# Products and their parts for two v tiles at a time, one-hots in two instructions, gate factors on ScalarE

## The reference

```
s_top, i_top = top_k(keys . (x @ w_q), 16)          # per head, two halves
best, pos = top_k(s_top[0] + s_top[1], 16)          # 16 of 16384 experts per head, 8 heads
g = softmax(best)
h = gelu(x . u[expert])
out = sum over the chosen experts of (g * h) * v[expert]
```

## Time and profile before

| what | us |
|---|---|
| median of 3 timed runs | 1654.39 |
| lowest and highest of them | 1652.92, 1654.40 |
| the profiled execution, span from its first to its last instruction | 1652.1 |
| PE busy | 1634.0 |
| DVE busy | 1246.6 |
| ACT busy | 646.1 |

### The profile page before, as it was taken

How to read it: one execution, slowest core, us unless ns; L and a number is a source line. 1 busy time by engine, 2 the same in 40 slices (tenths; PEclk the granted TensorE clock), 3 DMA queues, 4 the chain that set the end, 5 groups by cost and what they waited for, 6 DMA issues and landing times.

```text
span 1652.1 us, 23515 instructions
## 1 busy us (share of the span) xinstructions
PE 1634.0 (99%) x9093; PEld 1456.3 (88%) x9093; DVE 1246.6 (75%) x2357; ACT 646.1 (39%) x1006; POOL 464.2 (28%) x218
## 2 busy tenths in 40 slices
PE   9999999999999999999999999999999999999997
PEld 7898987888888999999999999999998888888886
DVE  3023456444799999998888789998998888888887
ACT  5333345543222343345545333333333433333332
POOL 4432223343224557410000223333333122222100
PEclk9999999999999999999999999999999999999999
DMA  5431112126112558588787999999999999999961
GB/s 204 157 140 52 52 54 77 45 83 230 52 52 82 182 176 295 190 330 279 242 281 237 350 390 394 380 388 370 358 375 375 390 384 375 375 363 386 399 242 70
DMA packets 135135, 407.05 MB, mean 246 GB/s; under 512 B 10352, under 2 KB 71024, under 8 KB 113776
## 3 DMA queue, kind: packets, MB, share of 16 engines
q1 hardware_dynamic: 116592, 271.32, 45.1%
q0 software_dynamic: 18432, 134.23, 20.7%
HBM read 360.94 MB, written 44.56 MB: 245 GB/s over the span
## 4 chain that ended last, share of the span: by engine, by line
PE 81%; DVE 17%; DMA 1%; issue 1%; ACT 0%; DVEq 0%; SPq 0%
PE bank L1303 24%; PE bank L1305 24%; PE bank L1304 24%; PE bank L1585 3%; PE bank L1422 2%; DVE idx L1084 1%; DVE idx L1076 1%; DVE val L1075 1%; DVE val L1083 1%; DVE tmp L1077 1%; PE bank L1437 1%; DVE prod L1140 1%; PE bank L1393 1%; PE bank L1385 1%; DVE prod L1149 1%
## 5 line engine op out<-in xcount | busy, mean ns | idle before, releaser
L1303 PE MATMUL bank<-xhi,whi 128*128 128x384 f32 (+1 forms) x1408 | 499.5, 355 | 2.3 <-ACT hout L824 1.8
L1305 PE MATMUL bank<-xhi,wlo 128*128 128x384 f32 (+1 forms) x1408 | 492.7, 350 | 0.0
L1304 PE MATMUL bank<-xlo,whi 128*128 128x384 f32 (+1 forms) x1408 | 492.0, 349 | 0.0
L629 POOL DMA_INDIRECT uvb<-in_uv,eidx x128 | 201.6, 1575 | 697.8 <-DVE acc L1191 667.4
L803 ACT ACTIVATE whi<-raw 128x1024 fp32r<-128x1024 f32 x256 | 270.2, 1057 | 254.4 <-PE bank L1305 228.1
L1169 DVE TENSOR_TENSOR wlo<-raw,whi 128x1024 fp32r<-128x1024 f32 x218 | 265.9, 1221 | 78.9 <-ACT whi L803 78.2
L1305 PE MATMUL bank<-whi,alo 128*128 128x512 f32 x768 | 299.5, 390 | 0.0
L1304 PE MATMUL bank<-wlo,ahi 128*128 128x512 f32 x768 | 299.4, 390 | 0.0
L1303 PE MATMUL bank<-whi,ahi 128*128 128x512 f32 x768 | 298.7, 389 | 0.0
L1303 PEld LDWEIGHTS bank<-xhi,whi 128*128 128x128 f32 x1408 | 264.5, 188 | 18.8 <-issue 3.9
L1305 PEld LDWEIGHTS bank<-xhi,wlo 128*128 128x128 f32 x1408 | 264.3, 188 | 15.6
(11 more groups left out here) (202 smaller groups left out, 1848.2 us busy)
## 6 DMA issues: line engine op xcount, KB each, us to landing
raw<-in_u SPq DMA_DIRECT2D x128, 512.0 KB
raw<-in_uv SPq DMA_DIRECT2D x128, 512.0 KB
g_scratch<-stage SPq DMA_DIRECT2D x48, 512.0 KB, 5.1
gl<-g_scratch SPq DMA_DIRECT2D x32, 768.0 KB
raw<-in_w_in SPq DMA_DIRECT2D x22, 1024.0 KB, 4.8
h_scratch<-hout SPq DMA_DIRECT2D x88, 192.0 KB, 5.3
hl<-h_scratch SPq DMA_DIRECT2D x22, 768.0 KB, 10.1
raw<-in_w_q SPq DMA_DIRECT2D x6, 1024.0 KB, 4.7
```

Source lines behind the costliest of these rows:

```text
L629: nc.gpsimd.indirect_dma_start(out=uvb[:, k % UVB, :], out_offset=None, in_=a["uv"][:, :], in_offset=bass.IndirectOffsetOnAxis(ap=eidx[:, ...
L1303: mm(out, lh, rh, start=first, stop=False)
L1304: mm(out, lh, rl, start=False, stop=False)
L1305: return mm(out, ll, rh, start=False, stop=last)
```

## The change

It makes four edits. (1) `product`, `high_a` and `product_low` treat two v tiles p and p + 1 in one instruction of 768 elements instead of two of 384. The pair's product is put in `PAIR_STEP`: for p below 40 this is two steps after the u tile of p + 1. (2) ACT's `high_a` of a pair is issued in ACT's turn two steps ahead of DVE's, where it was three, and DVE's `product_low` comes two steps after the product, where it was one. (3) `one_hots` compares both index rows in one instruction and multiplies by both weight rows in one. (4) The gate factor of the gathered experts is applied by ACT with two instructions of one element for each partition, where DVE did it with one of two elements; DVE's `sums` waits for both.

```diff
+PAIR_STEP = []
+for p in range(0, NT, 2):
+    at_step = U_POS[v_tile(p + 1)] + 2 if p < FUSED else V_POS[p] - 1
+    PAIR_STEP.append(max(PAIR_STEP[-1:] + [at_step]))
-    at_step = U_POS[v_tile(p)] + 4 if p < FUSED else V_POS[p] - 1
...
                 act.wait_ge(dot_done, 2 * j + 2)
-                nc.scalar.activation(hgel[:, 2 * j:2 * j + 2], hd[:, 2 * j:2 * j + 2], ACT.Gelu).then_inc(dot_gelu, 1)
+                if j == 0:
+                    act.wait_ge(w_done, 1)
+                nc.scalar.activation(hgel[:, 2 * j:2 * j + 2], hd[:, 2 * j:2 * j + 2], ACT.Gelu).then_inc(gel_step, 1)
+                act.wait_ge(gel_step, j + 1)
+                for k in (2 * j, 2 * j + 1):
+                    nc.scalar.activation(hd[:, k:k + 1], hgel[:, k:k + 1], ACT.Copy, scale=wg[:, k:k + 1]).then_inc(dot_gelu, 1)
             def high_a(t):
-                act.wait_ge(a_done, t + 1)
+                act.wait_ge(a_done, t + 2)
                 if t >= 4:
-                    act.wait_ge(v_done, t - 3)
-                nc.scalar.activation(ahi[:, t % 4, :], af[:, t % 4, :], ACT.Copy).then_inc(a_hi, 1)
+                    act.wait_ge(v_done, t - 2)
+                nc.scalar.activation(ahi[:, t % 4:t % 4 + 2, :], af[:, t % 4:t % 4 + 2, :], ACT.Copy).then_inc(a_hi, 2)
...
-                for p in products_in(s + 3):
+                for p in pairs_in(s + 2):
                     high_a(p)
...
             def sums(j):
-                dve.wait_ge(dot_gelu, j + 1)
-                ks = slice(2 * j, 2 * j + 2)
-                step(V.tensor_tensor(hd[:, ks], hgel[:, ks], wg[:, ks], ALU.mult))
+                dve.wait_ge(dot_gelu, 2 * j + 2)
...
-                V.tensor_tensor(e2[:, b % 2, :, :, :], numbers, per_token(1), ALU.is_equal)
-                if b >= 1:
-                    dve.wait_ge(e_done, b)
-                step(V.tensor_tensor(e1q[:, :, :, :], numbers, per_token(0), ALU.is_equal))
-                V.tensor_tensor(e1w[:, b % 2, 0, :, :, :], e1q[:, :, :, :], per_token(2), ALU.mult)
-                V.tensor_tensor(e1w[:, b % 2, 1, :, :, :], e1q[:, :, :, :], per_token(3), ALU.mult).then_inc(e_done, 1)
+                numbers = iota2[:, :, :].unsqueeze(1).to_broadcast([P, 8, P, 2])
+                step(V.tensor_tensor(e12[:, b % 2, :, :, :, :].rearrange("p n g e t -> p (n g) e t"), numbers, per_token(0), ALU.is_equal))
+                ones = e12[:, b % 2, 0, :, :, :].unsqueeze(1).to_broadcast([P, 2, 4, P, 2])
+                V.tensor_tensor(e1w[:, b % 2, :, :, :, :].rearrange("p n g e t -> p (n g) e t"), ones.rearrange("p n g e t -> p n g (e t)"), per_token(2), ALU.mult).then_inc(e_done, 1)
...
             def product(p):
                 if p < FUSED:
-                    dve.wait_ge(h_gelu, n + 1)
-                    h = hout[:, n % 4, :]
+                    dve.wait_ge(h_gelu, n + 2)
+                    h = hout[:, n % 4:n % 4 + 2, :]
...
             def product_low(p):
-                dve.wait_ge(a_hi, p + 1)
+                dve.wait_ge(a_hi, p + 2)
...
-                for p in products_in(s - 1):
+                for p in pairs_in(s - 2):
                     product_low(p)
```

More of the change, by code:

```diff
@@ L115, in v_tile, with pairs_in @@
     return (FIRST_FUSED + p) % NT
-PRODUCT_STEP = []
-for p in range(NT):
-    at_step = U_POS[v_tile(p)] + 4 if p < FUSED else V_POS[p] - 1
-    PRODUCT_STEP.append(max(PRODUCT_STEP[-1:] + [at_step]))
-def products_in(step):
-    return [p for p in range(NT) if PRODUCT_STEP[p] == step]
+PAIR_STEP = []
+for p in range(0, NT, 2):
+    at_step = U_POS[v_tile(p + 1)] + 2 if p < FUSED else V_POS[p] - 1
+    PAIR_STEP.append(max(PAIR_STEP[-1:] + [at_step]))
+def pairs_in(step):
+    return [p for p in range(0, NT, 2) if PAIR_STEP[p // 2] == step]
 BW = S + 3 + 2 * P
@@ L282, in program @@
         arena.phase(at_work)
-        pickT = arena.buf("pickT", [P, 4, DT], F16)
+        pickT = arena.buf("pickT", [P, NB, 4, 8], F16)
         iota2 = arena.buf("iota2", [P, P, 2], F16)
-        e2 = arena.buf("e2", [P, 2, 4, P, 2], F16)
-        e1q = arena.buf("e1q", [P, 4, P, 2], F16)
+        e12 = arena.buf("e12", [P, 2, 2, 4, P, 2], F16)
         e1w = arena.buf("e1w", [P, 2, 2, 4, P, 2], F16)
@@ L562, in _ @@
                     sp.dma_start(ln2b[:, :], a["ln2_b"].partition_broadcast(P)).then_inc(ln2_in, 16)
-                for p in products_in(s):
+                for p in [p + 1 for p in pairs_in(s)]:
                     if p % 4 == 3:
@@ L1220, in product @@
                         dve.wait_ge(h_in[n // 4 % 2], 16 * (n // 8) + 16)
-                    h = hl[:, n // 4 % 2, n % 4, :]
-                V.tensor_tensor(af[:, p % 4, :].rearrange("p (s t) -> p s t", s=SETS), h.rearrange("p (s t) -> p s t", s=SETS),
-                                gl[:, p // 4 % 2, :, p % 4, :], ALU.mult).then_inc(a_done, 1)
+                    h = hl[:, n // 4 % 2, n % 4:n % 4 + 2, :]
+                V.tensor_tensor(af[:, p % 4:p % 4 + 2, :].rearrange("p n (s t) -> p n s t", s=SETS),
+                                h.rearrange("p n (s t) -> p n s t", s=SETS),
+                                gl[:, p // 4 % 2, :, p % 4:p % 4 + 2, :].rearrange("p s n t -> p n s t"),
+                                ALU.mult).then_inc(a_done, 2)
             def product_low(p):
-                dve.wait_ge(a_hi, p + 1)
-                V.tensor_tensor(alo[:, p % 4, :], af[:, p % 4, :], ahi[:, p % 4, :].bitcast(F32), ALU.subtract).then_inc(a_lo, 1)
+                dve.wait_ge(a_hi, p + 2)
+                two = slice(p % 4, p % 4 + 2)
+                V.tensor_tensor(alo[:, two, :], af[:, two, :], ahi[:, two, :].bitcast(F32), ALU.subtract).then_inc(a_lo, 2)
             def norm_last(c, part):
@@ L1272, in _ @@
                     dots(j)
-                for p in products_in(s):
+                for p in pairs_in(s):
                     product(p)
@@ L1279, in _ @@
                     dve.wait_ge(pt_done, 3)
-                    step(V.tensor_copy(pickT[:, 0, :], bank[0][:, 0:DT]))
-                    step(V.tensor_copy(pickT[:, 1, :], bank[1][:, 0:DT]))
-                    step(V.tensor_scalar(pickT[:, 2, :], bank[2][:, 0:DT], W_SCALE, None, ALU.mult))
-                    V.scalar_tensor_tensor(pickT[:, 3, :], bank[2][:, 0:DT], W_SCALE, pickT[:, 2, :], ALU.mult, ALU.subtract).then_inc(pt_out, 1)
+                    by_batch = [bank[n][:, 0:DT].rearrange("p (b t) -> p b t", t=8) for n in range(3)]
+                    step(V.tensor_copy(pickT[:, :, 0, :], by_batch[0]))
+                    step(V.tensor_copy(pickT[:, :, 1, :], by_batch[1]))
+                    step(V.tensor_scalar(pickT[:, :, 2, :], by_batch[2], W_SCALE, None, ALU.mult))
+                    V.scalar_tensor_tensor(pickT[:, :, 3, :], by_batch[2], W_SCALE, pickT[:, :, 2, :], ALU.mult, ALU.subtract).then_inc(pt_out, 1)
                     dve.wait_ge(pt_out, 1)
@@ L1584, in g_quad @@
                     for w in range(2):
-                        last = mm(g_bank(q)[:, i * P:(i + 1) * P], e2[:, b, g, :, t], e1w[:, b, w, g, :, t], start=w == 0, stop=w == 1)
+                        last = mm(g_bank(q)[:, i * P:(i + 1) * P], e12[:, b, 1, g, :, t], e1w[:, b, w, g, :, t], start=w == 0, stop=w == 1)
                 last.then_inc(g_done, 1)
```

8 lines of the change are left out of this document (4 added, 4 removed).

## The result

The changed kernel takes 1664.26 us (median of 4 runs, 1660.07 to 1667.16) against 1654.06 (4 runs, 1652.92 to 1654.4): a ratio of 1.0063, 95% interval 1.0047 to 1.0079. It is slower, and by more than the range of the prediction allowed. The profiled execution is the fastest of the four, 1660.07 us, with a span of 1658.2 against 1652.1.

A forecast was written before the change was run, and what follows sets the result against it. PE was taken as the bound, busy 1634.0 of 1652.1 us. Terms -0.15 + 3.2 + 0.8 gave +3.9, so 1656.0 us for the profiled execution and, 2.3 above, a median of 1658.3 us; range 1653.9 to 1661.5.

The forecast's parts named there:

- The first one-hots: First two one-hot batches and the gathered pairs ahead of them: -0.15 us, between -0.6 and +0.5.
- The start of the products: Steps 91 to 97, first pair product waiting for the gelu of u tile 89: +3.2 us, bounds 0 to some +8.
- PE waits 1.9 us: Before u tile 92, near 970: PE waits for the late gelu of u tile 90, 1.9 us.
- the two signs: Would prove it wrong: gelu of u tile 89 before 963.5, or gate copies costing DVE well over 0.15 us.
- PE waits 1.4 us more: Step 97, near 992: PE waits 1.4 us for `tile_low(97)`, forecast to end at 992.25.
- The end: Last v tiles: `alo` of 126 and 127 comes behind `tile_low(255)`, delaying PE by +0.8 us, bounds +0.4 and +0.95.
- The v-only steps: V-only steps before the end: `product_low` a step later is covered by 5.5 us more room, so nothing was counted.
- The alternating stage: Where u and v tiles alternate: DVE keeps some 3 us of slack at its tightest and catches up slowly.
- From span to median: The runs' median was taken to stand 2.3 us above the profiled span, turning 1656.0 into 1658.3 us.
- the delay that feeds itself: Rival: late `sums` and low parts make loads late, adding one more load wait, 1662 to 1663 us; chance 0.12.
- The wide one-hots: Rival: one-hots run at half rate, each instruction 1.07 us longer, PE waits 64 us, 1718 us; chance 0.04.
- the faster case: Rival: DVE's saving reaches PE's waits at 688 and 723; 1652.7 us, below 1651.1 only without both waits; chance 0.08.

The follow-up runs named there:

- e2: Changed kernel with the one-hot and gate edits undone, so pairs only, against the kernel before: 1658.48 us, ratio 1.0029.
- e3: Kernel before with each `product_low` one step later and nothing paired: 1654.89 us, ratio 1.0012 to the kernel before.
- e9: Changed kernel with its gate edit alone undone (gates multiplied on DVE again): 1657.7 us, ratio 1.0027 to the kernel before.
- e10: e7 with the gate edit undone, leaving pairs and two-instruction one-hots: 1655.14 us, ratio 1.0005 to the kernel before.
- e6: Changed kernel with, in the v-only steps, the high part ahead of `tile_high` and the low part one step earlier: 1657.81 us, ratio 1.0026 to before.
- e4: The changed kernel run again, unaltered: 1660.15 us, ratio 1.0052 to the kernel before.
- e5: Changed kernel with the first pair's product in step 92 instead of 91, its low part in 93: 1659.16 us, ratio 1.0036 to the kernel before.
- e8: Changed kernel without the loads of stored gelu values after the first two (later v tiles use old values): 1660.31 us, ratio 1.0043 to the kernel before.
- e7: Changed kernel with the edits of both e5 and e6: 1654.68 us, ratio 1.0009 to the kernel before.
- e11: e7 with the first four gathered pairs moved to steps 50, 56, 62 and 68: 1650.24 us, ratio 0.9978 to the kernel before.
- e1: Kernel before with only the one-hot and gate edits, no pairs: 1653.87 us, ratio 1.0004 to the kernel before.

## Why the prediction was wrong

**The first one-hots**: -0.15 forecast, -0.28 measured. That is not shown to be right: e2 and e3, in which neither the gates nor the one-hots are changed, have -0.72 and -0.57 at the same step, and e9 and e10, which are the same program up to there, -0.99 and +0.91. A term of 0.15 cannot be read out of single traces that scatter so. What the traces do show are the sizes: two batches take DVE 4.88 us (720.90 to 725.78) where before they took 5.15 and I had 4.9, and a one-hot instruction is 1.22 us (1.23 forecast), an `alo` 0.951 (0.95). PE's later start at step 37 is swallowed by DVE's chain, as I had it. (The change as printed above has `p n g (e t)` in the line of `e1w`; the kernel has `p n (g e t)`. The order of the elements is the same, and the rate was kept.) The Trainium skill, VectorE: DVE Perf Modes, "The TRN2 errata", has many small tiles pay a fixed cost that a large one pays once; the trace agrees, 0.951 us against two of 0.552. Only my total for DVE was too large: 43 us of durations became 25.1 of busy time. Neighbours on the queue overlap by 0.09, and with 224 instructions merged away that much more is lost: some 20 us, by my estimate.

**The start of the products**: +3.2 forecast, 3.42 in the profiled execution, 4.12 to 4.35 in the other three that have this order and the gates' copies. The step "PE waits 1.9 us" was right (1.86, same chain), and so was the end of `tile_low(97)`, 992.25 against 992.16. In part that was luck. The gelu of u tile 89 came at 962.77 and not at 963.49, one of the two signs that I had named as proving me wrong, and the other held too: the copies cost twice what I had. From the gelu's end at 968.01 to `sums` at 968.57 are 0.56 us, where I had 0.38 and before had 0.23: 0.33 a pair instead of 0.15, since a copy takes 0.287 us and not 0.20. The two errors nearly cancel; where the gelu came later, the term is larger by up to 0.9.

"PE waits 1.4 us more" did not happen in this form: the half clock made PE 1.67 later by itself, and it arrived as `tile_low(97)` ended. In this place the clock cost nothing of its own: between 963.40 and 992.16 nothing on DVE's chain waits for PE, and in e2 and e9, where the clock stayed at 1.0, PE stood 0.98 and 0.97 us at step 97 instead.

**The end**: +0.8 forecast, 0.93 measured. Right in kind and nearly in size, and e6 takes it away by the order alone.

**The v-only steps: the first step that failed.** I wrote that there PE has 5.5 us more of cover than at the end, "I count nothing". It cost 2.11 us in the fastest execution, 0.23 to 1.90 in e2, e4, e5 and e9, 0.35 in e8, and 0.00 in all four kernels that put the order back (e6, e7, e10, e11). The cover was computed with tiles that arrive in time. I had two load waits in front of me (4.41 us, and a mean DMA share of 0.95), and used them for the start of the products alone. The order of before let a late load delay only its own tile, which had four steps of room. The new one puts the current product behind that tile, on ACT and on DVE.

**The alternating stage.** I wrote that DVE has "some 3 us of slack at its tightest" there and forecast no wait behind step 97. That held in every trace but e8's, where one load came late and steps 161 and 162 cost 3.90 us.

**From span to median: the second step that failed, and the larger one.** I added 2.3 us, as before. The changed kernel's median lies 6.1 above the profiled span. e4 ran the same kernel again and has its median at 1660.15, 1.9 above its span and inside my range, so this part of the miss is executions that differ. e8's is the only slow one with a trace (1662.81), and its late load explains it. The runs of the changed kernel well above 1660 may be such late loads, but they have no trace, and e2, e6 and e10 do not fit one cause of the scatter: it stays open.

The sum for the profiled execution was 3.9 and is 6.18: -0.13 (first), +0.22 (start), +0.13 (end), +2.11 (v-only) are the 2.3 between them, within rounding. The other 3.8 us of the miss are the median's. Of the rivals, the delay that feeds itself came nearest in size, with another mechanism: load waits passed on by the queue's order, while the delay itself feeds nothing, as e6 shows. The wide one-hots kept their rate, and the faster case failed as reasoned, since DVE's saving mostly fell beside PE's work.

## What to carry to other kernels

Merging two instructions moves the first one's work later and ties it to the second one's input (in e8 the product of one tile waited for the gelu of the next, behind a late load); before counting what the merge saves, list what now stands ahead of it on each queue, above all instructions that wait for a transfer. Cover worked out from a trace where loads land in time is no cover where the DMA share is 0.95: subtract the longest load wait that the trace shows. And where an engine at 74% busy makes the bound engine wait, first see whether its work can stand elsewhere: here four moved pairs gave 4 us, and 288 fewer instructions nothing.

## What the runs showed of the hardware

TensorE's granted clock fell to 0.5 (1.2 GHz) behind some of PE's waits in full-speed stretches, each time for 3.41 us, which made PE 1.5 to 1.7 us later at the next step. It did so behind all five waits of 1.86 to 2.05 us (step 92 in the changed kernel, e4, e6 and e8; step 161 in e8). At step 37 it did not go by length alone: with 2.34 us it fell in the changed kernel, e1, e5 and e7, but not in e4, e6 and e8; with 1.83 or 1.84 it fell in e2 and e3, but not in before, e9 and e10. Behind waits up to 1.66 us it never fell. At step 37 the loss is swallowed by DVE's chain up to the first one-hots, as a missing wait on `e1w` in those traces shows.

The landing time of a 512-KB tile load varied by several us from one execution of the same program to another, with the DMA share at 0.9 and more: the wait near 1250 is 3.29 us in the changed kernel's trace, 3.39 in e4's, 8.53 in e8's, which up to there is the same program. All three are for the tile of step 161.
